# Gated linear attention inside a transformer block: 128-token chunks made of two 64-token ones, states kept at 128-token borders only

## The reference, cut to what matters

```
b = cumsum(g within a chunk);  b_last = b at the chunk's last token
q_dec = q * dk**-0.5 * exp(b);  k_dec = k * exp(-b);  k_end = k * exp(b_last - b)
scores = where(causal, q_dec @ k_dec.T, 0)            # 64 x 64 per chunk
kv     = k_end.T @ v                                  # 128 x 256 per chunk
state[n] = exp(b_last[n]) * state[n-1] + kv[n]        # scan over the chunks
o = scores @ v + q_dec @ state_before_the_chunk
y = o * rsqrt(mean(o*o) + eps) * norm_w * silu(r)
```

## Time and profile before

| | us |
|---|---|
| median of three runs | 874.74 |
| span of the profiled execution, first to last instruction | 873.0 |
| device time outside that span, median less span | 1.7 |
| PE busy | 859.7 (98%) |
| PE weight loads busy | 715.1 (82%) |
| DVE busy | 297.8 (34%) |
| ACT busy | 314.4 (36%) |
| POOL busy | 337.9 (39%) |
| DMA, mean | 103 GB/s |

### The profile page before, as it was taken

How to read it: one execution, slowest core, us unless ns; L and a number is a source line. 1 busy time by engine, 2 the same in 40 slices (tenths; PEclk the granted TensorE clock), 3 DMA queues, 4 the chain that set the end, 5 groups by cost and what they waited for, 6 DMA issues and landing times.

```text
span 873.0 us, 10397 instructions
## 1 busy us (share of the span) xinstructions
PE 859.7 (98%) x4078; PEld 715.1 (82%) x4078; DVE 297.8 (34%) x304; ACT 314.4 (36%) x313; POOL 337.9 (39%) x80
## 2 busy tenths in 40 slices
PE   8999999999999999999999999999999999999996
PEld 7888888788788888888888898888888888888885
DVE  6374428563473912121212333000000000444445
ACT  3532445654655623232322553222222222222233
POOL 4444443214224244444444525444444444444440
PEclk9999999999999999999999999999999999999999
DMA  8842212212112132222225212222222222222212
GB/s 322 270 174 96 98 49 97 72 72 96 38 58 96 47 98 96 96 96 96 96 96 217 96 50 97 96 96 96 96 96 96 96 96 96 97 96 96 96 48 97
DMA packets 14658, 89.82 MB, mean 103 GB/s; under 512 B 1712, under 2 KB 1968, under 8 KB 5296
## 3 DMA queue, kind: packets, MB, share of 16 engines
q1 hardware_dynamic: 12384, 82.32, 26.1%
q10 hardware_dynamic: 2256, 7.24, 2.4%
HBM read 87.46 MB, written 2.10 MB: 103 GB/s over the span
## 4 chain that ended last, share of the span: by engine, by line
PE 92%; DVE 3%; ACT 2%; issue 1%; DMA 1%; POOL 0%; DVEq 0%; ACTq 0%; POOLq 0%
PE bank L849 19%; PE bank L851 19%; PE bank L850 19%; PE bank L868 9%; PE bank L867 9%; PE bank L866 9%; PE bank L1009 1%; PE bank L995 1%; PE bank L1003 1%; PE bank L965 1%; DVE vgs L649 1%; DMA par<-cols 1%; PE bank L895 0%; ACT w_hi L306 0%; PE bank L896 0%
## 5 line engine op out<-in xcount | busy, mean ns | idle before, releaser
L259 POOL TENSOR_TENSOR w_lo<-raw,w_hi 128x2048 fp32r<-128x2048 f32 x71 | 327.1, 4607 | 484.9 <-ACT w_hi L306 484.9
L849 PE MATMUL bank<-xt_hi,w_hi 128*128 128x512 f32 (+1 forms) x704 | 269.6, 383 | 3.2 <-ACT yb L406 1.5
L851 PE MATMUL bank<-xt_hi,w_lo 128*128 128x512 f32 (+1 forms) x704 | 267.1, 379 | 0.0
L850 PE MATMUL bank<-xt_lo,w_hi 128*128 128x512 f32 (+1 forms) x704 | 267.1, 379 | 0.0
L306 ACT ACTIVATE w_hi<-raw 128x2048 fp32r<-128x2048 f32 x72 | 137.7, 1912 | 297.3 <-PE bank L851 157.1
L849 PEld LDWEIGHTS bank<-xt_hi,w_hi 128*128 128x128 f32 x704 | 132.4, 188 | 29.5 <-issue 3.2
L850 PEld LDWEIGHTS bank<-xt_lo,w_hi 128*128 128x128 f32 x704 | 132.4, 188 | 25.8 <-issue 1.0
L851 PEld LDWEIGHTS bank<-xt_hi,w_lo 128*128 128x128 f32 x704 | 132.4, 188 | 25.1
L790 DVE TENSOR_TENSOR act<-bank,sil 128x512 f32 (+1 forms) x22 | 15.2, 692 | 199.2 <-PE bank L851 199.2
L795 DVE TENSOR_TENSOR al<-act,ah 128x1024 fp32r<-128x1024 f32 x11 | 51.7, 4700 | 60.2 <-ACT ah L504 60.2
L866 PE MATMUL bank<-w_hi,ah 128*128 128x512 f32 x176 | 68.5, 389 | 0.0
(11 more groups left out here) (175 smaller groups left out, 950.6 us busy)
## 6 DMA issues: line engine op xcount, KB each, us to landing
raw<-wstream SPq DMA_DIRECT2D x72, 1024.0 KB, 4.8
xw<-x_t SPq DMA_DIRECT2D x4, 512.0 KB, 8.2
h<-x ACTq DMA_DIRECT2D x1, 2048.0 KB, 7.8
out<-h SPq DMA_DIRECT2D x3, 512.0 KB, 2.6
raw<-wstream SPq DMA_DIRECT2D x2, 512.0 KB, 5.8
xn_in<-x SPq DMA_DIRECT2D x2, 512.0 KB, 12.0
xn_in<-x ACTq DMA_DIRECT2D x2, 512.0 KB, 4.3
vbias_bc<-vbias ACTq DMA_DIRECT2D x1, 1024.0 KB, 7.8
```

What stands on the lines that cost most here:

```text
L259: pool.tensor_tensor(w_lo[s][:, :], raw[s][:, :], w_hi[s][:, :], ALU.subtract).then_inc(lo_ready, 1)
L849: pe.matmul(dst, wh[:, k, cs], rh[:, k, ts], start=(k == 0), stop=False)
L850: pe.matmul(dst, wh[:, k, cs], rl[:, k, ts], start=False, stop=False)
L851: last = pe.matmul(dst, wl[:, k, cs], rh[:, k, ts], start=False, stop=(k == KD - 1))
```

## The change

GLA is computed on 128-token chunks composed of two 64-token ones, without a change of the exponents' range. Three states (at tokens 128, 256, 384) are kept in place of seven. DVE multiplies each pair of decay factors (`pair_decay`), makes `kx` (the first half's keys as the second half sees them), scales the first half's `k_end` by the second half's decay so that one 128-row product gives the pair's kv, and, once the scores are done, scales the second half's queries by the first half's decay (`later`, semaphore `q_joined`) so that one state serves both halves. PE computes four more score blocks, `kx` by the second half's queries, into the off-diagonal 64 x 64 squares of bank 5; the mask is filled there by a memset. The kv products become three of 128 rows, and the state products six of 128 columns.

```diff
-KV_BANKS = (2, 3, 4, 5)
+KV_BANKS = (2, 3, 5)
...
-        state = sb("state", 188, [P, NCH - 1, DV])
+        state = sb("state", 188, [P, TT - 1, DV])
+        kx = sb("kx", 191, [P, TT, CHUNK])
...
+        pair_decay = sb("pair_decay", 207.53125, [P, TT])
...
             v.wait_ge(causal_landed, 16)
+            v.memset(causal_f[0:CHUNK, CHUNK:P], 1.0).then_inc(causal_joined, 1)
+            v.wait_ge(causal_joined, 1)
             v.tensor_copy(causal[:, :], causal_f[:, :]).then_inc(causal_set, 1)
...
                 v.tensor_copy(decay.unsqueeze(2), expb[:, :, CHUNK - 1:CHUNK]).then_inc(decayed, 1)
-                v.wait_ge(decayed, i * 4 + 1)
+                v.wait_ge(decayed, i * 7 + 1)
+                ends = decay.rearrange("p (t c) -> p t c", c=2)
+                v.tensor_tensor(pair_decay[:, :].unsqueeze(2), ends[:, :, 0:1], ends[:, :, 1:2], ALU.mult).then_inc(decayed, 1)
...
+                halves = rest[:, :, :].rearrange("p (t c) s -> p t c s", c=2)
+
+                v.tensor_tensor(kx[:, :, :], qk[:, bass.ds(i + HEADS, 1), :].rearrange("p a (t s) -> p (a t) s", s=P)[:, :, 0:CHUNK],
+                                halves[:, :, 0, :], ALU.mult).then_inc(decayed, 1)
+                v.wait_ge(decayed, i * 7 + 4)
+                v.tensor_tensor(halves[:, :, 0, :], halves[:, :, 0, :], ends[:, :, 1:2].broadcast_to([P, TT, CHUNK]), ALU.mult
+                                ).then_inc(decayed, 1)
+                v.wait_ge(decayed, i * 7 + 5)
                 v.tensor_tensor(rest[:, :, :], kh, rest[:, :, :], ALU.mult).then_inc(decayed, 1)
...
+                later = expb[:, :, :].rearrange("p (t c) s -> p t c s", c=2)[:, :, 1, :]
+                v.tensor_tensor(later, later, ends[:, :, 0:1].broadcast_to([P, TT, CHUNK]), ALU.mult).then_inc(q_joined, 1)
+
+                for n in range(TT - 1):
+                    v.wait_ge(kv_done, i * 3 + (n + 1))
+                    kv = bank[KV_BANKS[n]][:, 0:DV]
                     if n == 0:
                         v.tensor_copy(state[:, 0, :], kv).then_inc(state_ready, 1)
                     else:
-                        v.wait_ge(state_ready, i * 7 + n)
-                        v.scalar_tensor_tensor(state[:, n, :], state[:, n - 1, :], decay[:, n:n + 1], kv,
+                        v.wait_ge(state_ready, i * 3 + n)
+                        v.scalar_tensor_tensor(state[:, n, :], state[:, n - 1, :], pair_decay[:, n:n + 1], kv,
                                                ALU.mult, ALU.add).then_inc(state_ready, 1)
...
-                pe.wait_ge(decayed, i * 4 + 4)
+                pe.wait_ge(decayed, i * 7 + 7)
...
+                for t in range(TT):
+                    mm = pe.matmul(bank[5][0:CHUNK, t * P + CHUNK:(t + 1) * P], kx[:, t, :], expb[:, 2 * t + 1, :],
+                                   start=True, stop=True)
                 mm.then_inc(scores_done, 1)
                 gate_tile(1, 1)
...
-                for n in range(NCH - 1):
-                    if n >= 4:
-                        pe.wait_ge(state_ready, i * 7 + (n - 3))
-                    r0 = (n % 2) * CHUNK
-                    mm = pe.matmul(bank[KV_BANKS[n % 4]][:, 0:DV],
-                                   ken[r0:r0 + CHUNK, n // 2, :], vst[r0:r0 + CHUNK, n // 2, :], start=True, stop=True)
-                    if n % 2 == 1 or n == NCH - 2:
-                        mm.then_inc(kv_done, 1)
-
+                for n in range(TT - 1):
+                    pe.matmul(bank[KV_BANKS[n]][:, 0:DV], ken[:, n, :], vst[:, n, :], start=True, stop=True
+                              ).then_inc(kv_done, 1)
+
+                pe.wait_ge(q_joined, i + 1)
                 for q in range(2):
                     qs = slice(q * P, (q + 1) * P)
                     for t in range(TT):
-                        pe.matmul(bank[6 + q][:, t * P:(t + 1) * P], vst[:, t, qs], sct[:, t, :],
-                                  start=(t == 0), stop=(t == 0), skip_group_check=True)
-                        for n in (2 * t, 2 * t + 1):
-                            if n > 0:
-                                if q == 0:
-                                    pe.wait_ge(state_ready, i * 7 + n)
-                                mm = pe.matmul(bank[6 + q][:, n * CHUNK:(n + 1) * CHUNK], state[:, n - 1, qs], expb[:, n, :],
-                                               start=False, stop=True, skip_group_check=True)
+                        ts = slice(t * P, (t + 1) * P)
+                        mm = pe.matmul(bank[6 + q][:, ts], vst[:, t, qs], sct[:, t, :],
+                                       start=(t == 0), stop=(t == 0), skip_group_check=True)
+                        if t > 0:
+                            if q == 0:
+                                pe.wait_ge(state_ready, i * 3 + t)
+                            mm = pe.matmul(bank[6 + q][:, ts], state[:, t - 1, qs],
+                                           expb[:, 2 * t:2 * t + 2, :].rearrange("p c t -> p (c t)"),
+                                           start=False, stop=True, skip_group_check=True)
                     mm.then_inc(o_done, 1)
```

More of the change, by code:

```diff
@@ L177, in build @@
         eps_set, keep_set, ones_set, sct_zeroed = sem("eps_set"), sem("keep_set"), sem("ones_set"), sem("sct_zeroed")
-        causal_set, seen = sem("causal_set"), sem("seen")
+        causal_set, causal_joined, seen = sem("causal_set"), sem("causal_joined"), sem("seen")
+        q_joined = sem("q_joined")
         swt_masked = sem("swt_masked")
@@ L689, in _ @@
                                   bank[5][:, :].rearrange("p (t s) -> p t s", t=TT)).then_inc(sct_ready, 1)
-                for n in range(NCH - 1):
-                    if n % 2 == 0:
-                        v.wait_ge(kv_done, i * 4 + (n // 2 + 1))
-                    kv = bank[KV_BANKS[n % 4]][:, 0:DV]
+                later = expb[:, :, :].rearrange("p (t c) s -> p t c s", c=2)[:, :, 1, :]
[3 more added lines that the diff above has]
+                    kv = bank[KV_BANKS[n]][:, 0:DV]
                     if n == 0:
```

## The result

The changed kernel takes 869.36 us (median of four runs, 869.32 to 869.42) against 874.75 before: 5.39 us less, a ratio of 0.9939 with a 95% interval of 0.9927 to 0.995. The span of its profiled execution is 867.7 us against 873.0. The forecast was 869.5.

A forecast was written before the change was run, and what follows sets the result against it. PE's ordered list was taken as the bound, 92% of the chain of waits. Gains of 4 x 1.67 us less 3 x 0.47 for new scores give 5.27, so 874.74 - 5.27 = 869.5 us, range 866.5 to 871.6.

The forecast's parts named there:

- PE from K on: PE's kv, output and mix records would take 1.4 + 3.16 + 1.84, reaching the sum of squares 3.3 us sooner.
- K: Start of a head's kv matmuls on PE, 170.77 us in the first head; other times are counted from it.
- the hold: DVE's addition of two SBUF squares, blocked by POOL's pass, ends 0.55 us after it; gain 1.67 a head, not 3.3.
- The wait in its place: Before the sum of squares, PE idles 1.5 us for DVE's addition (line 715), which lands in POOL's pass.
- POOL's pass against K: POOL's `w_lo` pass stays at K+2.80 to K+7.32; if it moves, the prediction is wrong.
- The scores: Four new score matmuls ahead of K, eight records at 0.058: 0.47 us a head in heads 2 to 4.
- the cover: First head: PE's 1.54 us idle for ACT's silu hides DVE's additions and new score matmuls, with 0.2 us left.
- DVE's additions, `q_joined`, the memset: DVE work, 1.0 to 1.2 us ahead of the scores, a later query product and memset: all hidden, no cost.
- After the last head: At the mixers' results, `yb_lo` keeps 0.63 of its 0.80 us slack, so the heads' gain reaches the end whole.
- No hold: Rival: the addition slips past POOL, PE never waits, a head gains 3.3 us; 862.9 us, chance 0.10.
- The clock: Rival: PE's idling drops its clock to 1.2 GHz for one projection, 5.7 us a head; 892.2 us, chance 0.03.
- The third: Rival: DVE's queue behind the addition makes PE wait for `decayed`, path not shortened; 874 to 875 us, chance 0.04.

The follow-up runs named there:

- the bank version: Changed kernel with ACT's second square written to bank 5 instead of SBUF and read there by DVE's addition: 861.67 us, ratio 0.9851.
- the first three experiments: Changed kernel with, separately, the second square in a bank (861.67 us), second-slot `w_hi` made behind the squares (861.67), half of POOL's pass (862.02).

## Why the prediction was right

Both the sign and the size held for the reason given; the terms, in the order of the prediction:

- **PE from K on.** Forecast 1.4 + 3.16 + 1.84 = K+6.4; measured 1.29 + 3.12 + 1.79 (the last in the bank version), K+6.2. The tenth for the start did not appear: six records at 0.215 us are 1.29. The error of 0.2 us had no effect, because it lay under the hold. The states were in time. The prediction's "0.113 whatever its columns" holds between 64 and 128 columns only; its own rows have 0.43 us for 512.
- **The wait in its place.** This was the step that made the difference between 862.9 and 869.5. Forecast: the addition ends at K+7.87 and PE starts at K+7.92. Measured: K+7.94 and K+8.00. The offset of 0.55 us behind POOL's end, taken from line 754, came out to 0.01. The duration was 2.70 us for about 2.5, since the addition came 0.16 sooner than forecast (K+5.24 for K+5.4) and the pass ended 0.07 later against K. PE's wait and restart together cost 1.9 us a head by the bank version; the forecast had said 1.6 (3.3 less 1.67), most of the difference being the 0.2 on PE's list.
- **POOL's pass against K.** The prediction named a move of this pass as a sign of being wrong. It did move, from K+2.80 and K+7.32 to K+2.88 and K+7.39, and the reason given for its place still holds: it hangs on the end of `gate_tile(1,1)`, and K came nearer to that. The last projection record starts 0.31 us ahead of K before (170.46) and 0.23 after (170.55). That PE starts the sum 0.08 us later against K, and that K lies about 0.08 us nearer to the projection, are two small errors of the forecast that cancel; the agreement to 0.14 us in the total is in part luck.
- **The scores.** Forecast 0.47 a head in heads 2 to 4; the chain of waits has 0.46 us for the eight new records, 0.058 each, and leaving them out gave 1.32 us for 1.4. The 0.058 was a choice between two bounds, not a reading. In the first head the cover held with 0.24 us to spare (forecast 0.2).
- **Ledger.** The sum of squares moved by 180.46 - 178.78 = 1.68 us in the first head; a period of 32.50 for 33.73 adds 1.23 for each further head; 1.68 + 3 x 1.23 - 0.10 for the restart in the last is 5.27 (the restarts of the others lie within the period). The median moved by 5.39, the span by 5.3. The 1.8 us a head at the top of the forecast's range was given without a row.
- **DVE's additions, `q_joined`, the memset.** No cost. The run with DVE's products alone shows it for them, and in PE's list of waits `decayed` shows once, in the first head, and `q_joined` never. The products lengthen DVE's work from the scan to `cum` by 0.93 us in the first head (forecast 1.0 to 1.2). The memset takes 0.11 us, and the idle time behind it shrinks from 13.07 to 12.89. The product behind `q_joined` was held by POOL in heads 2 to 4 as forecast, and is done 1.9 us ahead of K.
- **After the last head.** `yb_lo` is done 0.62 us ahead of PE (forecast 0.63), so nothing was given back. That `yb_lo` was itself held before is not in the earlier trace rows, but the trace has it: POOL's pass runs from 296.70 to 301.35 there, and the product of the same shape in front of it (line 736) takes 2.29 us for 6.70.
- **The rivals.** "No hold" is what the first three experiments produce: 861.7 to 862.0, against 862.9 forecast. The clock stayed at 1.00 in spite of waits of 1.6 us in every head. The third did not occur.

What a reader could take for granted and is not so: PE was busy 98% of the time, the change took 3.5 us a head off its list, and the result kept under half of that. The new scores took about 1.4 us in all, and the hold 7.7. The page of the profile shows none of it; the order of two rows did, line 715 at K+8.68 and the end of a pass on another engine at K+7.32.

## What to carry to other kernels

Before crediting an engine with work removed, move each instruction behind that work to its new time and see what runs on the other engines then; here a VectorE operation that had just missed a GpSimd pass moved into it. Where a VectorE instruction with two SBUF inputs stands near a long GpSimd pass, as lines 729, 705 and 754 do here, its place in time is part of its cost. Putting one operand in a bank, or moving the pass, may be worth more than the change itself: here 7.7 us against 5.4. Idle time elsewhere is a resource for added work, but only where a row shows it and for as long as that row says.

## What the hardware showed that was not expected

- Small plain-float32 matmuls with weights of 128 columns cost 0.112 us a record at 64 and at 128 columns alike (48 more records: 5.40 us). Those with weights of 64 columns that all write the same half of the partitions cost 0.058 at 64 columns (eight records in 0.46 us).
- Two 64-row matmuls on different halves of the rows run together (0.01 us apart), but going from full height to half and back costs about 0.4 us in all (1.73 us over four heads).
- A held VectorE operation ends sooner after POOL's pass than its duration alone: 0.28 us against 0.41 for 256 elements, 0.55 against 0.69 for 512, 2.15 against 2.29 for 2048 (`yb_lo`, before). The difference is 0.13 or 0.14 us at every size, so the operation does not work faster; a fixed part of its duration lies within the hold. Which part that is, no run here shows.
